# A decoder layer with a product-key expert layer: the first block's scatter put between the projection's last items, the eight decode tokens moved to the end

## What is computed

```python
def one_block(xb):                                   # 128 tokens
    q = (xb @ w_q).reshape(PEER_BLOCK, PEER_HEADS, 2, PEER_DK_HALF)
    s = jnp.einsum('thcd,hcnd->thcn', q, keys)
    sv, si = lax.top_k(s, PEER_TOPK)                 # 16 of 128 keys, twice a head
    cand = sv[:, :, 0, :, None] + sv[:, :, 1, None, :]
    cv, ci = lax.top_k(cand, PEER_TOPK)              # 16 of 256 pairs
    eid = i0 * PEER_N_KEYS + i1                      # 8 heads x 16 = 128 experts a token
    gate = jax.nn.softmax(cv, axis=-1)
    u = w_down[eid]
    act = jax.nn.gelu(jnp.einsum('td,thkd->thk', xb, u))
    return jnp.einsum('thk,thkd->td', gate * act, w_up[eid])
```

## Time and profile before

| | us |
|---|---|
| median of 3 runs | 3515.72 (3501.64 to 3517.16) |
| the profiled execution | 3514.68 |
| its span, from first to last instruction | 3512.9 |
| PE matmuls busy | 3152.1 (90%) |
| DVE busy | 2615.6 (74%) |
| POOL busy | 1632.5 (46%) |
| ACT busy | 773.4 (22%) |
| bytes moved | 1077.16 MB, mean 307 GB/s |

### The profile page before, as it was taken

The page is one execution under the profiler, slowest core; times in us unless marked ns, Lnnn a source line. Parts: engine busy times, 40 slices in busy tenths (PEclk is TensorE's granted clock), DMA queues, the critical chain, the costliest instruction groups (busy, mean ns, idle before and its releaser), DMA issues.

```text
span 3512.9 us, 33177 instructions
## 1 busy us (share of the span) xinstructions
PE 3152.1 (90%) x11349; PEld 1837.6 (52%) x11349; DVE 2615.6 (74%) x5082; ACT 773.4 (22%) x2004; POOL 1632.5 (46%) x1269
## 2 busy tenths in 40 slices
PE   8998898987979987755889999999999999999977
PEld 5766777756737652442444543544544544543422
DVE  2397336877878787686699999999999975876640
ACT  2002542213210111250340420430430420420000
POOL 0000002443444677553356665665665764765520
PEclk9999999998987998857999999999999999999999
DMA  4111556887798999977899999999999999999997
GB/s 133 36 36 67 179 180 238 303 318 261 267 339 284 361 386 397 360 248 280 301 360 384 350 356 395 345 371 386 335 382 385 334 395 370 367 376 410 409 358 222
DMA packets 328859, 1077.16 MB, mean 307 GB/s; under 512 B 40524, under 2 KB 76941, under 8 KB 328028
## 3 DMA queue, kind: packets, MB, share of 16 engines
q0 software_dynamic: 172416, 625.03, 47.4%
q1 hardware_dynamic: 121515, 428.89, 33.4%
q10 hardware_dynamic: 34760, 21.14, 1.9%
HBM read 1052.50 MB, written 23.94 MB: 306 GB/s over the span
## 4 chain that ended last, share of the span: by engine, by line
PE 37%; DMA 21%; DVE 18%; issue 9%; POOL 4%; ACT 2%; ACTq 1%; DVEq 0%; POOLq 0%
PE psum L1526 27%; DMA arena<-in_w_up 13%; DVE arena L1780 7%; DMA arena<-in_w_down,arena 4%; POOL arena L1282 3%; PE psum L1519 3%; DVE arena L1798 2%; PE psum L1488 2%; DMA arena<-in_w_q 2%; PE psum L1365 1%; ACTq L2010 1%; PE psum L1367 1%; PE psum L1465 1%; DVE arena L1741 1%; DVE arena L1743 1%
## 5 line engine op out<-in xcount | busy, mean ns | idle before, releaser
L1282 POOL DMA_INDIRECT arena<-in_w_down,arena x1024 | 1419.9, 1387 | 1004.8 <-DVE arena L1780 763.2
L1526 PE MATMUL psum<-arena 128*128 128x512 f32 x3584 | 1628.9, 602 | 95.0 <-DMA arena<-in_w_up 91.0
L1780 DVE CUSTOM_DVE_ANT_0 arena<-arena 128x1024 f32<-128x1024 f32 x1024 | 1214.8, 1221 | 172.7 <-DMA arena<-in_w_down,arena 165.9
L1526 PEld LDWEIGHTS psum<-arena 128*128 128x128 f32 x3584 | 655.8, 192 | 925.2 <-issue 662.0
L1365 PE MATMUL psum<-arena 128*128 128x256 f32 (+2 forms) x1536 | 367.1, 394 | 27.6 <-DVE arena L1681 16.6
L2075 ACT ACTIVATE arena<-arena 128x128 f32<-128x128 f32 x896 | 285.7, 390 | 373.2 <-DVE arena L1798 370.2
L1798 DVE TENSOR_TENSOR arena<-constants,arena 128x1024 f32<-128x1024 f32 x224 | 272.0, 1221 | 108.1 <-ACT arena L2064 57.5
L1519 PEld LDWEIGHTS psum<-arena 128*128 128x128 f32 x1792 | 255.3, 209 | 181.2 <-ACT arena L2075 105.3
L1519 PE MATMUL psum<-arena 128*128 128x128 f32 x1792 | 265.1, 297 | 78.8 <-ACT arena L2075 78.7
L1365 PEld LDWEIGHTS psum<-arena 128*128 128x128 f32 x1536 | 272.6, 198 | 111.9 <-DVE arena L1681 18.9
L284 PE MATMUL psum<-arena 128*128 128x344 f32 x816 | 238.4, 455 | 3.0 <-DVE arena L324 3.0
(11 more groups left out here) (253 smaller groups left out, 2184.8 us busy)
## 6 DMA issues: line engine op xcount, KB each, us to landing
arena<-in_w_up SPq DMA_DIRECT2D x512, 512.0 KB, 6.7
arena<-in_w_gates SPq DMA_DIRECT2D x96, 768.0 KB, 5.7
arena<-in_w_o SPq DMA_DIRECT2D x40, 512.0 KB, 6.7
arena<-in_w_q SPq DMA_DIRECT2D x32, 512.0 KB, 5.8
arena<-in_w_down,arena POOLq DMA_INDIRECT x1024, 8.1
arena<-in_w_chunks SPq DMA_DIRECT2D x26, 512.0 KB, 3.5
arena<-scratch_s POOLq DMA_DIRECT2D x64, 128.0 KB, 7.2
arena<-in_xT SPq DMA_DIRECT2D x4, 1032.0 KB, 7.8
```

The costliest lines, as they stand in the source:

```text
L1282: pool.indirect_dma_start(dst, None, table, bass.IndirectOffsetOnAxis(ap=idN[:, min(n, NT - 1) % 2, j:j + 1], axis=0)).then_inc(here, 16)
L1526: mm = pe.matmul(psum[:, 2 * (m % 2) + h, :], coef_block(m, s % NKEYS), wup[:, s % WUPR, h * 512:(h + 1) * 512], start=first, stop=end)
L1780: dve.tensor_tensor_reduce(row, row, rowD[slot_of["x", n]], 1.0, 0.0, ALU.mult, ALU.add, dots[:, n % 3, j:j + 1]).then_inc(row_used, 1)
```

## The change

Four things move.

1. **Block 0's scatter goes between the items.** A new item `ids0` turns block 0's expert numbers and coefficients four pairs before the last one; the 32 scatters stand behind parts of the last group's items: one behind each of the 16 parts of the two output projections, two behind each of `turn` 5 and 6, one behind each of the 8 query halves, one behind each of four scores. The items after the last pair use three bank pairs in turn, and the scatter keeps the fourth.
2. **Its coefficients go where columns are dead.** At that time the eight places of 32 expert blocks are still in use; block 0's 128 go to columns of `hT` and of the branches that no later item reads, in four runs instead of two, so that `evacuate` has four ACTIVATEs. To free the places, ring buffers 3 and 10 to 12 close at row 270 instead of 250 and 320.
3. **The sample's broadcast, gathers and product move to passes 6 and 7.** `xbc` is loaded behind slice 38 of pass 6, `sdown` waits for the end of pass 5, and the product stands at step 56 of pass 7 (`SUP_AT`).
4. **The planner places the last sums too.** `sum` 5, `sum` 6, their norms and the sample's steps are put between block 7's `up` instructions, when its model finds them due.

```diff
-        items += scores([3, 4]) + pr[4:] + pairs_of(3, 1, 2)
+        items += scores([3, 4]) + pr[4:] + pairs_of(3, 1, 2)[0:12] + [("ids0",)] + pairs_of(3, 1, 2)[12:]
...
+        turn0 = items.index(("ids0",))
+        bank, prev_in = [], {}
+        for k in range(NI):
+            bank.append(2 * (k % 4 if k <= last_pair[3] else (0, 1, 3)[(k - last_pair[3] - 1) % 3]))
+            prev_in[k] = max((p for p in range(k) if bank[p] == bank[k]), default=-1)
+        SCATTER_BANK = 4
+        last_there = max(k for k in range(NI) if bank[k] == SCATTER_BANK)
+        woven = {}
+        for k in range(last_pair[3] + 1, NI):
+            if opens_set(k):
+                woven.update({(k, i): 1 for i in range(KD)})
+            elif items[k] in (("turn", 5), ("turn", 6)):
+                woven[k, 0] = 2
+            elif items[k][0] == "query":
+                woven.update({(k, i): 1 for i in range(2)})
+            elif items[k] in scores([XS, 5]):
+                woven[k, 0] = 1
+        assert sum(woven.values()) == NBATCH
+        last_query = max(k for k in range(NI) if items[k][0] == "query")
...
-        CSLOT = [(3, 4, 5, 2), (6, 7, 0, 1), (3, 4, 5, 0), (1, 2, 3, 6), (7, 3, 4, 5), (0, 1, 6, 7), (2, 3, 4, 6)]
...
+            if n == 0:
+                return [(at(0, KD, T)[:, :, 0:4 * P].rearrange("p k (e n) -> p k e n", n=P), 0, (KD, 4)),
+                        (at(12504, KD, T)[:, :, 0:5 * P].rearrange("p k (e n) -> p k e n", n=P), 32, (KD, 5)),
+                        (at(20760, 25, P), 72, (25,)),
+                        (at(8256, 31, P), 97, (31,))]
...
-        open_to = [SLOTS * (NT + 1)] * 3 + [250, 116] + [SLOTS * (NT + 1)] * 5 + [320] * 3
+        open_to = [SLOTS * (NT + 1)] * 3 + [270, 116] + [SLOTS * (NT + 1)] * 5 + [270] * 3
...
+            if sevac_next < NBATCH and m.done("scated", sevac_next):
+                m.put("sevac", sevac_next)
+                m.end["sevaced", sevac_next] = m.on_act(m.now, 1.7)
+                sevac_next += 1
+                continue
+            if dot_next == SLOTS * (NT + 1) and not last_put and m.end["up", SLOTS - 1] + 3.0 <= m.now:
+                m.put("last")
+                last_put = True
+                continue
...
-            if sum_next < DENSE - 2 and m.end.get(("passeded", sum_next + 1), m.now + 1) <= m.now:
+            if sum_next < DENSE and m.end.get(("passeded", sum_next + 1), m.now + 1) <= m.now:
...
+            if any(x[0:2] == ("scat", hot_next) for x in m.ops[m.at:m.at + (6 if hot_next < NBATCH else 1)]) and \
+                    m.done("turned", hot_next // NBATCH) and m.pe <= m.now + 6.5 and (hot_next < 2 or m.done("scated", hot_next - 2)):
...
+                    {"slist": head_next % 2 == 0, "sdown": m.done("passeded", DENSE - 2), "ssum": m.done("suped", 0),
+                     "sdot": m.end.get(("steped", (DENSE - 1, 38)), m.now) + 16.0 <= m.now}.get(next_sample, True):
...
-                sp.wait_ge(item_done, NI)
+                sp.wait_ge(item_done, last_query + 1)
...
-                for b in range(NB):
-                    sp.dma_start(xbc[:, b, :], bass.AP(tensor=scratch_xn.tensor, offset=(SEQ + b) * D, ap=[[0, P], [1, D]]))\
-                      .then_inc(xbc_here, 16)
...
+                    if i == 38 and k == DENSE - 1:
+                        for b in range(NB):
+                            sp.dma_start(xbc[b], bass.AP(tensor=scratch_xn.tensor, offset=(SEQ + b) * D, ap=[[0, P], [1, D]]))\
+                              .then_inc(xbc_here, 16)
...
-                        pool.wait_ge(item_done, NI)
-                        for b in range(2):
-                            pool.wait_ge(xb_out[b], 16 * (NX // 2 + (b < NX % 2)))
+                        pool.wait_ge(step_done, HALF * (DENSE - 1))
...
+                def scatter(n, q):
+                    g = NBATCH * n + q
+                    pair = (hot if n else hot0)[:, g % 2]
+                    pe.wait_ge(hot_ready, g + 1)
+                    if g >= 2:
+                        pe.wait_ge(scat_copied, g - 1)
+                    else:
+                        released(last_there)
+                    for t in range(BATCH):
+                        mm = pe.matmul(psum[:, 4 + g % 2, t * P:(t + 1) * P], pair[:, 1, t, :], pair[:, 0, t, :],
+                                       start=True, stop=True)
+                    mm.then_inc(scat_done, 1)
+
+                scattered = [0]
+
+                def weave(k, part):
+                    for _ in range(woven.get((k, part), 0)):
+                        scatter(0, scattered[0])
+                        scattered[0] += 1
...
-                turn(0)
-                for q in range(NBATCH):
-                    scatter(0, q)
...
+                        if i == SUP_AT and n == DENSE:
+                            pe.wait_ge(y_sum, DENSE - 1)
+                            pe.wait_ge(smask, NB + 1)
+                            pe.wait_ge(rowS_here, 16 * 2 * NB)
+                            for b in range(NB):
+                                for h in range(2):
+                                    mm = pe.matmul(psum[0:NB, 2 + h, :], cmask[:, b, :], rowS[b][:, h * 512:(h + 1) * 512],
+                                                   start=(b == 0), stop=(b == NB - 1))
+                            mm.then_inc(sup, 1)
...
+                def first_evacuate():
+                    act.wait_ge(row_used, max(drained.values()))
+                    for u in range(5):
+                        act.wait_ge(x1_out[u % 3], 16 * (u // 3 + 1))
+                        for i in range(2):
+                            scores_out(act, u, i)
...
+                    elif s[0] == "sevac":
+                        if s[1] == 0:
+                            first_evacuate()
+                        evacuate(0, s[1])
```

339 lines of the change are left out of this document (191 added, 148 removed).

## The result

The changed kernel takes 3535.38 us (median of 5 runs, 3520.16 to 3544.7), the kernel before 3515.72 (5 runs): a ratio of 1.0063 with a 95% interval of 1.0040 to 1.0085. It is some 20 us slower, a little more than the 0.5% that can be told. The forecast was 3495, 20 us faster. The profiled execution took 3544.7 with a span of 3542.9, against 3514.7 and 3512.9 before, so the traces differ by 30 us; the profiled execution of after was 9 us over its median.

A forecast was written before the change was run, and what follows sets the result against it. PE was taken to bound the dense passes, DVE and DMA close behind. PE's end, 3505.2 - 97 - 33 + 8 + 18 = 3401, plus a 91 us tail gave span 3492, forecast median 3495, range 3455 to 3542.

The forecast's parts named there:

- a): Before pass 0: block 0's scatter leaves its own stretch, 97 us won, bounds 0 and 129.
- b): Pass 0 without the sample's product and transfers: 33 us won, bounds 14 and 38.
- c): Passes 1 to 5: PE bounds them and does the same, 0 us; bounds 0 and 27 us gained.
- rival 1: Dense passes: PE is tied to the rows, its lead 71 us instead of 130, span 3551; chance 0.15.
- d): Pass 6: eight broadcast loads ahead of slices lose 8 us, bounds 0 and 16.1; `sdown` is on no path.
- e): Pass 7: the sample's product at step 56 and more gathers beside it lose 18 us, bounds 12 and 25.
- f): The tail behind PE's end: 91 us instead of 7.7, with `up` at 1.55 us; bounds 79 and 114.
- rival 3: Tail slower: `up` and issues take turns (span 3531), or `sdown`'s hold reaches block 5's sum (3512); chance 0.25.
- g): After the items: the sample's lists go out on ACT's queue instead of SP's, at no cost.
- theory 2: Expectation for unwoven: the transfers set the end and only their idle time counts, 29 us, time 3564.

The follow-up runs named there:

- before_no_sample: The kernel before without the sample's lists, rows, dots, product, sum and norm, its output row only copied: 0.9936 of the kernel before.
- unwoven: The changed kernel with block 0's 32 scatters all behind the last item: 1.0101 of the kernel before.
- unwoven_last: The changed kernel with block 0's 32 scatters behind the last item and the last sums behind the last `up`: 1.0010 of the kernel before.
- before_2_scatters: The kernel before with only 2 of block 0's 32 scatters, the other 30 left out: 0.9889 of the kernel before.
- last_xbc_spread: sums_last with the eight broadcast loads one at every second slice of pass 6, and the sample's dots 14 slices later: 0.9919 of the kernel before.
- spread_both: last_xbc_spread with the sample's product ahead of step 24 of pass 7, its lists loaded early and `sdown` 24 rows later: 0.9907 of the kernel before.
- sums_last: The changed kernel with block 6's and the sample's sums and norms behind the 128th `up` and the last block's norm: 0.9952 of the kernel before.

## Why the prediction was wrong, by its own steps

The step that failed is the sum "3505.2 - 97 - 33 + 8 + 18 = 3401" for PE's end, which the trace has at 3464.0: it takes what PE gains at the front as time gained at the end. By the timed ratios the weaving, put at 97 us, was worth 20; the tail, put at 83 us more, cost 39; all the rest, put at 33 won and 26 lost, cost 4. The tail was overpriced and the weaving more so, and that turned the sign. That 3535 still lies within the stated 3455 to 3542 is the width of that range, and two errors against each other.

**a) failed.** "The stretch to grow by 32 us, so 129 - 32 = 97", under the rule of the first part that "everything before pass 0 that PE spends or waits counts in full, if the rest keeps pace". The start came 77 us earlier in this trace, the latest of the eight with this code (77 to 90), within the bounds. But 26 of these belong to the sample, and the weaving's own 51 to 65 us were worth 20 us at the end, 27 without the sample. The rest did not keep pace, and could not: beside PE's slices go the rows, 0.97 of the DMA engines' time in a dense pass. PE's lead is 13 slices in a pipeline where a slice costs 1.45 us to bring and 4.1 us to use, and pass 7 lasts 19 us longer for it. The same row that I read as "PE ends last there, with two others close behind" shows this bound as well; the sum priced only the first of the three. Why PE still waited in the woven stretch: 12 times, 36.5 us in all, for one-hots that DVE makes between dots and evacuations. I had counted their time as fitting beside PE by adding busy times, which says nothing of their order.

**b) half of it.** Pass 0 shrank by 19 us, not 33, and another 26 us of the sample stood in the stretch before it, which I had put to the scatter. Together that is 53 us by the start of pass 1 in before_no_sample. But the sample's place was worth nothing at the end that can be told: 22 us early or late. The 33 and 53 us were again leads of PE's.

**c) outside its bounds.** I had 0 to 27 us gained; it was 15 lost. Passes 1 to 5 took 1299 to 1313 us in the eight kernels with this code and 1291 to 1297 in four without the weaving (before, before_no_sample, unwoven, unwoven_last), but 1308 in before_2_scatters, where PE is early too. An early PE waits a little more: for scaling 11.9 us instead of 2.5 in unwoven_last, for slices 26.5 instead of 23.1. This is a trace of rival 1 (PE tied to the rows), not its size.

**d) too small.** 21 us, not 8, and above the bound of 16: the eight loads in front of a slice cost PE one wait of 20.6 us and not the 10 us of their bytes; 9 gathers went through the same full DMA engines in it. At 16.1 us to landing the upper bound was the better reading. Spread out, pass 6 is 12.5 us shorter. That `sdown` is on no path was right by its run; DVE did wait 16.0 us the other way, for PE at block 5's sum.

**e) right:** 20 us for 18.

**f) right in kind, a little high:** 71 us more behind PE for 83. Without PE's slices the `up` ran at DVE's speed:

```profile
L1955 DVE SCALAR_TENSOR_TENSOR arena<-arena 128x1024 f32<-128x1024 f32 x53 | 68.1, 1285 | 1.8
L1345 POOL DMA_INDIRECT arena<-in_w_up,arena x46 | 48.5, 1054 | 27.0 <-DVE arena L1955 13.6 <-issue 13.4
```

53 `up` have 1.8 us of idle time before them in all. In the 72 us DVE was busy for 68.1 and POOL's 46 issues for 48.5, so at least 44 us of them overlap. This settles rival 3 in its first form: a row does not cost an `up` and an issue one after the other.

The overlap is not free for POOL, though. Two pairs from the same trace (start, length, what):

```profile
3321.75 0.94 POOL L1345 DMA_INDIRECT arena<-in_w_up,arena  x1 [0.30 <-issue]
3321.91 1.29 DVE L1955 SCALAR_TENSOR_TENSOR arena<-arena 128x1024 f32<-128x1024 f32 x1 [1.28 <-DMA arena<-in_w_up,arena]
```
```profile
3325.91 2.60 DVE L1955 SCALAR_TENSOR_TENSOR arena<-arena 128x1024 f32<-128x1024 f32 x2 [0.15 <-DMA arena<-in_w_up,arena]
3326.03 1.98 POOL L1345 DMA_INDIRECT arena<-in_w_up,arena  x1 [1.62 <-DVE arena L1955]
```

The issue that starts 0.16 us ahead of an `up` takes 0.94 us. The one that starts 0.12 us inside an `up` takes 1.98: it ends 0.81 us after that `up`, while the next one runs. So it is everywhere in this trace: of 74 issues begun inside an `up` with over 0.2 us of it left, 72 end 0.80 to 0.85 us behind its end, and of 467 begun inside a dot, 455; the 92 issues during which DVE does nothing take 0.93 to 0.97 us, and so do the 56 begun inside a MAX8 (one operand in SBUF) and the 10 inside the instruction of L1757 (one operand in SBUF, one in PSUM). The `up` have their usual 1285 ns beside an issue. In the tail most issues start 0.2 us before an `up` ends and so lose only 0.08 us each, which is why the rows still come at DVE's pace. The Trainium skill (SBUF — State Buffer, "SBUF: two separate sides") has a DVE instruction with two SBUF inputs and a POOL operation that reads SBUF hold their shared ports in turn. This trace agrees for a first part of an issue, which waits for the end of an `up` or a dot (both read SBUF twice) and not of the others; it does not agree for the issue's whole length, since its last 0.81 us run beside the next `up`.

The tail's price for the end is lower than 71: putting the sums behind costs PE 30 us of pass 7, so the tail cost 39.

**g) right:** no wait for the lists is seen at the front.

So the terms against these two traces, with the chance in them: a 20 us short, b 14, c 15, d 13, e 2, f 12 the other way. That makes 52 of the 51 us between the forecast span's change (-21) and the measured one (+30). The fault is in leads of one engine added up as time.

**The rivals.** The first, PE tied to the rows, was nearest in size (a span of 3551 for 3543; its lead of 71 us where the forecast had 130 is near the 82 us that PE had at pass 6). Its mechanism, PE waiting at the one-hots, is seen only in c's few us; the lead went later, to the sample's work and to the rows beside pass 7. The third was right that the tail costs more than the front wins, and wrong on what it costs an `up`.

## Which version to take

The weaving is worth keeping, the sums' place among the last `up` is not. last_xbc_spread and spread_both, at 0.9919 and 0.9907, beat both kernels: 28 and 33 us under the kernel before, 50 and 55 under the changed one.

## What to carry to other kernels

Where two streams share a resource that is nearly full, don't add up one engine's leads: count the units that each has done at a common time (here 0.5 MB slices and rows), and value a lead by what it has moved. What fits these runs is that an overlap gains the idle time of the shared resource that it fills: 29 us by unwoven's theory 2, 20 and 27 measured. And a wait put into an in-order queue cost nothing to be seen while the ring behind it took it up; once the ring was full it cost in proportion to the items left behind it, 39 us for 58 rows and 21 for 28. Ask how many are left there at the time the wait ends.

## What the runs showed of the hardware that was not expected

POOL's issue of a gather takes 0.93 to 0.97 us while DVE is idle. Begun inside a DVE instruction that reads two rows of 128x1024 from SBUF (an `up` of 1285 ns, a dot of 1222), it nearly always ends 0.81 us after that instruction, up to 2.0 us in all, with its last part beside the next one; DVE is not slowed. One that starts just ahead of such an instruction is not held. In the tail both ran side by side at 1.32 us a row.

One of these gathers of 0.5 MB takes some 1.3 us of all DMA engines at 388 to 405 GB/s, the rate of pass 7 in sums_last; in passes 1 to 5 of the changed kernel slices and gathers move 354 to 371 GB/s at a share of 0.94 to 0.98. Eight broadcast loads of one 4 KB row into 128 partitions, one behind the other in one queue, landed 2.6 us apart beside the gathers, and PE waited 20.6 us for the slice behind them, twice what their 4 MB take alone at that rate.
